# First and last expert turn reordered, eight row sets summed by TensorE, one branch instead of a stage, l2 norms per token and head

## The reference, cut to what matters

```python
# first block, experts: each expert works on blocks of 128 rows
gu = xblk @ w_gate_up[e] + b_gate_up[e]
gate = jnp.minimum(gu[:, :D_EXPERT], SWIGLU_LIMIT)
up = jnp.clip(gu[:, D_EXPERT:], -SWIGLU_LIMIT, SWIGLU_LIMIT)
act = gate * jax.nn.sigmoid(SWIGLU_ALPHA * gate) * (up + 1)
yb = act @ w_down[e] + b_down[e]
y = jnp.zeros((T + 1, D)).at[row_tok].add(row_gate[:, None] * yb)
# between the blocks
x = rmsnorm(x + y, g_final); h = rmsnorm_2(x, g_pre) * (1 + scale) + shift
proj = h @ w_in
# second block, gated delta rule (4 heads of 128, chunks of 64)
qkv = silu(causal_conv(qkv, conv_w))
q = l2norm(heads(q, DK_A)) * (DK_A ** -0.5)
k = l2norm(heads(k, DK_A))
kb = k * beta[..., None]
lmat = where(strict, einsum('bhnik,bhnjk->bhnij', kb, k) * decay, 0)
attn = einsum('bhnik,bhnjk->bhnij', q, k) * decay
w = tmat @ (kb * exp(gc)); kg = k * exp(gc[-1:] - gc)
```

## Time and profile before

| what | value |
| --- | --- |
| median of three runs | 2097.52 us (2095.53 to 2098.78) |
| the profiled execution | 2097.29 us |
| its span, first to last instruction | 2095.5 us |
| TensorE busy | 1918.1 us (92%) |
| VectorE busy | 1534.8 us (73%) |
| ScalarE busy | 1127.9 us (54%) |
| GpSimd busy | 184.2 us (9%) |
| mean granted TensorE clock | 0.953 of full speed |
| DMA | 499.69 MB, mean 238 GB/s |

### The profile page before, as it was taken

How to read it: one execution, slowest core, us unless ns; L and a number is a source line. 1 busy time by engine, 2 the same in 40 slices (tenths; PEclk the granted TensorE clock), 3 DMA queues, 4 the chain that set the end, 5 groups by cost and what they waited for, 6 DMA issues and landing times. The chain is left out here.

```text
span 2095.5 us, 23964 instructions
## 1 busy us (share of the span) xinstructions
PE 1918.1 (92%) x8141; PEld 1363.1 (65%) x8142; DVE 1534.8 (73%) x1759; ACT 1127.9 (54%) x1172; POOL 184.2 (9%) x193
## 2 busy tenths in 40 slices
PE   6978978999999999999999999999979879979678
PEld 3345456777777777877777777777634334469443
DVE  4156667999989989989998999999732775654452
ACT  4333325777777777767777777777343451212231
POOL 0030310000000000000000000003410000023100
PEclk9988969999999999999999999999987999979899
DMA  6201747999999999999999999999752111010001
GB/s 201 80 9 70 283 159 268 346 373 383 347 373 361 380 366 355 383 347 377 363 369 379 358 377 358 378 380 354 262 176 77 40 41 40 0 61 4 19 1 40
DMA packets 94724, 499.69 MB, mean 238 GB/s; under 512 B 18498, under 2 KB 20783, under 8 KB 44403
## 3 DMA queue, kind: packets, MB, share of 16 engines
q1 hardware_dynamic: 87618, 473.37, 58.7%
q0 software_dynamic: 7056, 25.69, 3.5%
HBM read 478.57 MB, written 20.46 MB: 238 GB/s over the span
## 5 line engine op out<-in xcount | busy, mean ns | idle before, releaser
L1586 DVE TENSOR_TENSOR part<-ring,part 128x2048 fp32r<-128x2048 f32 x380 | 859.3, 2293 | 115.5 <-ACT part L1339 114.9
L1339 ACT ACTIVATE part<-ring 128x2048 fp32r<-128x2048 f32 x380 | 729.0, 1921 | 341.2 <-DMA ring<-in_w_gate_up 192.9
L1454 PE MATMUL bank<-part,xT_hi 128*128 128x512 f32 x2048 | 535.6, 404 | 24.6 <-DVE xT_lo L1615 24.5
L1454 PEld LDWEIGHTS bank<-part,xT_hi 128*128 128x128 f32 x2048 | 380.8, 190 | 121.8 <-issue 36.6
L1465 PE MATMUL bank<-part,actT_hi 128*128 128x512 f32 x1024 | 282.4, 398 | 4.0 <-issue 3.5
L1454 PE MATMUL bank<-part,xT_lo 128*128 128x512 f32 x1024 | 280.3, 395 | 0.0
L1454 PEld LDWEIGHTS bank<-part,xT_lo 128*128 128x128 f32 x1024 | 193.5, 189 | 45.8
L1465 PEld LDWEIGHTS bank<-part,actT_hi 128*128 128x128 f32 x1024 | 191.6, 190 | 46.3 <-issue 4.6
L2318 PE MATMUL bank<-ring 128*128 128x512 f32 x448 | 200.9, 609 | 8.0 <-PEq L166 7.8
L2318 PEld LDWEIGHTS bank<-ring 128*128 128x128 f32 x448 | 87.9, 197 | 121.8 <-issue 120.8
L1465 PE MATMUL bank<-part,actT_lo 128*128 128x512 f32 x512 | 160.3, 394 | 0.0
(11 more groups left out here) (447 smaller groups left out, 2168.7 us busy)
## 6 DMA issues: line engine op xcount, KB each, us to landing
ring<-in_w_gate_up SPq DMA_DIRECT2D x256, 1024.0 KB, 6.9
ring<-in_w_down SPq DMA_DIRECT2D x128, 1024.0 KB, 7.1
expert_rows<-rest SPq DMA_DIRECT2D x31, 512.0 KB, 7.7
ring<-in_w_in SPq DMA_DIRECT2D x7, 2048.0 KB, 8.8
rest<-in_w_ada SPq DMA_DIRECT2D x8, 1536.0 KB, 6.7
ring<-in_w_out SPq DMA_DIRECT2D x16, 512.0 KB, 6.3
ring<-in_w_in SPq DMA_DIRECT2D x8, 464.0 KB, 6.7
rest<-in_x SPq DMA_DIRECT2D x4, 512.0 KB, 5.5
```

Source lines behind the costliest of these rows:

```text
L1339: nc.scalar.activation(hi[c % PARTS], raw(c), ACT.Copy).then_inc(sig("hi_ready"), counts)
L1454: ins = nc.tensor.matmul(bank[g][:], rows[:, c, :], w[:, g * 512:(g + 1) * 512], start=first, stop=last, skip_group_check=True)
L1586: V.tensor_tensor(lo[c % PARTS], raw(c), hi[c % PARTS].bitcast(F32), ALU.subtract).then_inc(sig("lo_ready"), counts)
```

## The change

**Turn 0.** For expert 0, chunks 6 and 7 go into slots 2 and 3 (before: 0 and 1), as slots 0 and 1 are wanted by the next expert first. So the high parts of the next expert's chunks 0, 1 and 2 are made before the sigmoid, and VectorE makes the low part of the rows ahead of the last two steps of the activation.

```diff
+    def part(i, c):
+        return c - 4 if isinstance(i, int) and i == 0 and c >= PARTS else c % PARTS
...
-            make_hi(0, 6, 1, (0, 0))
-            make_hi(0, 7, 1, (0, 1), counts=1 + 4)
-            for c in (0, 1):
-                make_hi(1, c, 2, (0, c + PARTS))
+            make_hi(0, 6, 1, (0, 2))
+            make_hi(0, 7, 1, (0, 3), counts=1 + 4)
+            make_hi(1, 0, 2, (0, 0))
+            make_hi(1, 1, 2, (0, 1))
+            make_hi(1, 2, 2, (0, 6))
             sigmoid(0)
             copy_rows(2)
-            for c in (2, 3, 4, 5):
-                make_hi(1, c, 2, (0, c))
+            make_hi(1, 3, 2, (0, 7))
+            make_hi(1, 4, 2, (0, 4))
+            make_hi(1, 5, 2, (0, 5))
...
-            activate(0)
-            rows_lo(2)
+            activate(0, before_last=2)
```

```diff
-SUM_BANKS = (1, 2, 3, 0, 4, 5, 6, 7)
-BY_TENSOR = (7, 11, 14, 15)
+SUM_BANKS = (2, 3, 1, 0, 4, 5, 6, 7)
+BY_TENSOR = (6, 7, 9, 10, 11, 13, 14, 15)
...
             for c in (8, 9, 10):
                 down(i, c)
+            expert_bias(0)
+            expert_bias(1)
             turn_act(0, E)
...
+            make_lo(E, 8)
+            act_lo(0, E)
+            make_lo(E, 9)
+            act_lo(1, E)
+            for c in (10, 11):
                 make_lo(E, c)
-            act_lo(0, E)
-            make_lo(E, 11)
-            act_lo(1, E)
...
+            act_squares(nc, act, m, "", 0)
+            act_squares(nc, act, m, "", 1)
+            act_scaled(nc, act, m, "", 0)
+            act_scaled(nc, act, m, "", 1)
+            act_squares(nc, act, m, "", 2)
+            act_turned(nc, act, m, "", 0)
+            act_scaled(nc, act, m, "", 2)
+            act_squares(nc, act, m, "", 3)
+            for t in range(1, T):
+                ins = act_turned(nc, act, m, "", t)
```

```diff
         experts(nc, a, m)
-        retire("slot_loaded")
-        extra_experts(nc, a, m)
         retire("slot_loaded")
...
+    eng.wait_ge(m["sig"]("blocks_stored"), 1)
     return eng.value_load(m["extra_i"][0:1, MAX_EXTRA:MAX_EXTRA + 1], min_val=0, max_val=MAX_EXTRA)
```

```diff
-                M.matmul(bank[7][:], ones, square[:, n % 2, :], start=True, stop=True).then_inc(sig("qk_summed"), 1)
+                for t in range(T):
+                    at = 8 * t + n
+                    ins = M.matmul(bank[7][:, at:at + 1], square[:, n % 2, t * P:(t + 1) * P], ones[:, 0:1], start=True, stop=True, skip_group_check=True)
+                ins.then_inc(sig("qk_summed"), 1)
...
+            pool.wait_ge(sig("qk_var_ready"), 1)
+            nc.gpsimd.tensor_tensor(qk_scale, qk_var, half.unsqueeze(2).broadcast_to([P, T, 8]), ALU.pow).then_inc(sig("qk_root"), 1)
...
+                if gr == 0:
+                    pe.wait_ge(sig("scales_ready"), 1)
+                    pe.wait_ge(sig("relu_ready"), 3 * HI)
+                    for t in range(T):
+                        for h in range(HA):
+                            ins = M.matmul(bank[2 + t][:, h * P:(h + 1) * P], q_scale[:, t, h:h + 1].broadcast_to([P, P]), ident, start=True, stop=True, skip_group_check=True)
+                        ins.then_inc(sig("q_rows"), 1)
...
-                if 1 <= n <= 8:
-                    l2(n - 1)
                 choose(next(rounds))
-                if 1 <= n <= 8:
-                    l2_end(n - 1)
+                if n == 8:
+                    dve.wait_ge(sig("qk_summed"), 8)
+                    V.tensor_scalar(qk_var, bank[7][:, 0:32].rearrange("p (t n) -> p t n", t=T), EPS, None, ALU.add).then_inc(sig("qk_var_ready"), 1)
+            dve.wait_ge(sig("qk_root"), 1)
+            V.tensor_scalar(q_scale, q_scale, P ** -0.5, None, ALU.mult)
+            V.tensor_tensor(beta_k, beta, k_scale, ALU.mult).then_inc(sig("scales_ready"), 1)
...
-                chain.link(V.tensor_tensor(LT[:, t], heads(2), diff[:, t % 2], ALU.mult))
+                for h in range(HA):
+                    ins = V.scalar_tensor_tensor(out=LT[:, t, h, :], in0=heads(2)[:, h, :], scalar=k_scale[:, t, h:h + 1], in1=diff[:, t % 2, h, :], op0=ALU.mult, op1=ALU.mult)
+                chain.link(ins)
```

609 lines of the change are left out of this document (320 added, 289 removed).

## The result

Over eleven runs each the changed kernel took 2083.0 us (2075.05 to 2086.97) and the kernel before 2095.53 us (2084.89 to 2098.87): a ratio of 0.9938, 95% interval 0.9920 to 0.9957, or -13 us with -9 to -17 in the interval. It is faster, as forecast, and inside the range of 2068 to 2086, but 6.5 us above the forecast of 2076.5. The profiled execution of the changed kernel took 2084.2 us (span 2082.4).

The account below looks back on a forecast made before the run. Experts were taken as bound by TensorE with transfers just behind, the tile stage by VectorE's l2 norm. From 2097.3 us, -23.3 + 3.7 + 4.5 - 4.2 + 1.5 - 3.0 = -20.8 gave 2076.5 us, range 2068 to 2086.

Parts of the forecast that it names:

- Tile stage: Tiles of q and k without the l2 norm's work on VectorE: TensorE sets the pace, 7.8 us a tile, -23.3 us.
- q's products: Tile stage: 16 more small TensorE products spread q's factors, 0.234 us each, +3.7 us.
- rival 5: Tile stage: sums of squares cost 0.2 us instead of 0.9, and the boundary gives 4.2: 2070.4 us; chance 0.12.
- rival 1: l2 norms: GpSimd's roots come late, 2.26 us a column, 29 us on TensorE's path: 2105.8 us; chance 0.03.
- Chunks: Second block, four chunks: LT, AT and the decay of `kg` take VectorE longer while TensorE waits, +4.5 us.
- Boundary: Ahead of the second block: one barrier fewer shortens VectorE's wait, -3.0 us, bounds -2.2 and -4.2.
- First turn: Experts, turn 0: the activation starts earlier, at 328.4 instead of 332.6, -4.2 us, bounds -2 and -6.
- rival 2: Experts' loop: transfers cannot follow, so the first turn's gain is lost, +4.2, 2080.7 us; chance 0.13.
- End of the experts: Last turn and sums: `down` ends earlier, but TensorE's sums make the last variance ready later, +1.5 us.
- TensorE's list behind set 7: End of the experts: 24 products of 512 columns, 20.7 us, a turn of 0.94 and 1.9 for lower clock.
- rival 3: Sums ending the experts: TensorE spends half of its 24 products at 1.2 GHz, 2085 us; chance 0.11.
- How the numbers follow: Closing weights for the whole kernel: forecast 0.55, rivals 0.03 to 0.13, range 2068 to 2086, faster by over 0.2% 0.95.

Follow-up runs that it names:

- no_stage: The kernel before without the stage of extra blocks, its barrier and its clearing: 2091.3 us, ratio 0.9978 to the kernel before.
- experts_only: The changed kernel with the second block of before: 2095.38 us, ratio 0.9996 to the kernel before.
- turn0_only: The kernel before with the new first turn of the experts alone: 2092.39 us, ratio 0.9975 to the kernel before.
- filled_light: The changed kernel with unread products (2, 4, 1, 1) where TensorE waits in the second block: 2063.29 us, ratio 0.9836 to the kernel before.

## Why the prediction was right, and where it was off

Direction and range held; the forecast gain was 20.8 us and 13 were measured. By its own steps, against the stages of the two profiled executions and the experiments:

- **Tile stage, -23.3 with +3.7 for q's products: right.** -19.6 against -20.1. The two numbers behind it, 7.8 us a tile and 3.7 us for sixteen products, came out as 7.76 and 3.73, since each stood in a row of before. The price of a narrow product was the row's 0.12 us a record, 0.95 us for eight and not 0.2, so rival 5 fell with it; GpSimd's roots at 0.17 us a column were far under the 2.0 from which rival 1 would decide.
- **Chunks, +4.5: right**, +5.0 in the profiled pair, 4.3 with the clock held, and 4.4 for LT and AT alone (3.6 of the 4.5 had been put for these two).
- **Boundary, -3.0: right**, -3.3, and -3.0 in `no_stage`.
- **First turn, -4.2: right at its place, open at the end of the loop.** TensorE entered expert 1 at 333.65 instead of 337.72. The eight kernels with all of the new experts activate expert 0 on average 2.9 us earlier than the six others (one of which has the new first turn too), and expert 31 0.8 us later; experts 1 to 31 took 1113.9 us (standard error 1.5) against 1110.3 (1.0), one execution of each. That is what rival 2 (the transfers take the gain back) looks like, at 3.6 +- 1.8 us, and the time of `experts_only` agrees with it; that of `turn0_only`, -5.2 (-1.7 to -9), speaks against it. It is not settled.
- **End of the experts, +1.5: the right mechanism, too small.** From the last activation on, the stretch takes 57.0 us (five executions with eight sets) against 53.2 (six of the old order): +3.8. In the profiled pair it is +2.4, and there the mis-sized term can be read: TensorE's list behind set 7. Set 7 came when it was forecast (1512.3 less the 3.2 us by which expert 31 was earlier, against 1508.85), but from there to the end of the last product, 1533.31, it took 24.5 us, where 20.7 + 0.94 + 1.9 = 23.5 had been put. The low clock took 2.2 of it (1.9 had been put); the rest is in records a little above 0.43 us, as the four of a bias, which took 1.91 us. So rival 3's sign, a lower clock in the sums, did appear, for 5 of 48 records and not for half. Four sets in the new order take 51.8, 50.9 and 51.9 us: what cost time was the number of sets, not the order.
- **What was missing: +4.9 behind the chunks.** "How the numbers follow" let nothing happen behind the last changed instruction. I had a rival for a low clock at the sums (rival 3) and none for the stretches that have idle time in every turn, where the clock falls and rises again many times. Before, the logits had run at 0.78 and the outputs at 1.00, as these windows of the kernel before show; after, it was 0.74 and 0.92 (above).

```profile
1945.00:2016.00 71.00, 44.07 (x224) 34.48 (x222) 30.61 (x89) 17.89 (x48) 12.82 (x14) 0.78 0.00 1
2016.00:2054.00 38.00, 32.56 (x99) 16.08 (x99) 22.14 (x36) 12.41 (x21) 0.00 (x0) 1.00 0.00 1
```

The filled kernels show that it is clock: with products in the waits both stretches are as long in the old block as in the new one. Why the new block makes the clock fall more often in code that it does not touch is not shown. That the forecast still came out in its range is so because the terms that were right are large and the missing one is small.

Of the 7.7 us between -20.8 and the pair's -13.1, the clock behind the chunks is 4.9, the end of the experts 0.9 in this pair (2.3 by the means), the loop of experts with its first turn 1.1, the index scores 1.0; the first turn's -0.1, the chunks' 0.5, the tiles' -0.5, the boundary's -0.3 and 0.1 in the rest nearly cancel.

## What to carry to other kernels

A forecast from rows of the same shape held to a few tenths of a microsecond; the largest miss came from stretches whose code did not change. So list the stretches behind an edit in which TensorE idles a little in each turn, and ask what its clock does there: here such stretches were worth more (some 20 us) than the edit (13), since a few products in their waits kept the clock up. That worked where the waits were longer than the products (1.3 to 2.5 us in the logits, 0.86 us a product), and not in the index scores with their 0.2 us. And move work from the engine that is busy to the one that waits only as far as the wait reaches: with eight sets of rows TensorE ended the sums 5 us later than with four.

## What the hardware did that I had not expected

- The clock of TensorE stood at 0.50 for 22 us and more in a stretch in which it was busy for 20.11 of 22.00 us, and stayed at 1.00 in other executions with 19.87 of 22.00: 83 against 74 us for the same code.
- The fall of the clock repeated to a tenth of a microsecond between executions in one place (73.7 us of logits in three kernels, 71.0 in three others, whatever their start) and differed in another (the index scores: 74.0 us in three of the thirteen profiled executions that had no product added to every score, 81.6 to 83.7 in the others). Within one kernel it differs too: five executions of `filled_light` had a mean clock of 0.969 or 0.970, the sixth 0.977, and it was 11 us faster than the next (2049.27 and 2060.38 us). All three executions with 74.0 us have the old end of the experts (three of six; none of seven with the new one), which is too few to tell chance from cause: that the new end costs some of the 8.6 us is a rival that no run here settles.
- One added product of 512 columns in each wait of the logits raised the clock from 0.74 to 1.00 and made the stretch 13.7 us shorter, though nothing of its work changed.
